# Rebuilt token attention in a two-block transformer kernel: two score regions per lane, and the short key pieces of a differential step issued side by side

## The reference, cut to what matters

```
mod = silu(c) @ w_ada[l] + b_ada[l]          # shifts, scales, gates
A: p = softmax(q k^T * scale);              o = p v
B: p = softmax(q k^T * scale + window_bias); o = p v      # bias on the 512 token keys
C: p = softmax(q1 k1^T) - lam * softmax(q2 k2^T); o = rms_norm(p v) * g_sub   # differential
x  = x + gate * (concat(oa, ob, oc) @ w_out[l])
```

## Time and profile before

| | |
|---|---|
| median of 3 runs | 3680.66 us (3677.1 to 3681.37) |
| span of the profiled execution | 3674.5 us (the profile has no other time of this execution) |
| PE busy | 3542.3 us, 96% of the span |
| DVE, ACT, POOL busy | 47%, 42%, 40% |
| token attention, layer 0 and layer 1 | 241.7 to 475.6 us and 1346.6 to 1574.3 us |
| context attention, layer 0 | 521.9 to 586.1 us |

### The profile page before, as it was taken

The page is one execution under the profiler, slowest core; times in us unless marked ns, Lnnn a source line. Parts: engine busy times, 40 slices in busy tenths (PEclk is TensorE's granted clock), DMA queues, the critical chain, the costliest instruction groups (busy, mean ns, idle before and its releaser), DMA issues.

```text
span 3674.5 us, 50083 instructions
## 1 busy us (share of the span) xinstructions
PE 3542.3 (96%) x19796; PEld 2813.1 (77%) x19796; DVE 1740.4 (47%) x2922; ACT 1525.6 (42%) x2558; POOL 1458.9 (40%) x986
## 2 busy tenths in 40 slices
PE   7999898999999999899999989999999989999998
PEld 5776566888899776578887768878887768888886
DVE  5766634433344766633542686161114676162114
ACT  4445544433355446534332355443223345443222
POOL 4520023544488520035444435344444434434442
PEclk8999998999999999999999999999999999999999
DMA  7613512333365421523333213223333212313331
GB/s 229 159 48 116 172 47 69 98 98 96 94 183 173 122 54 36 161 84 97 98 95 98 75 35 100 85 71 97 97 96 79 75 41 81 103 58 102 94 98 58
DMA packets 642466, 355.59 MB, mean 97 GB/s; under 512 B 70469, under 2 KB 614841, under 8 KB 642233
## 3 DMA queue, kind: packets, MB, share of 16 engines
q1 hardware_dynamic: 630379, 339.66, 32.0%
q10 hardware_dynamic: 11854, 12.72, 1.2%
...
## 4 chain that ended last, share of the span: by engine, by line
PE 89%; DVE 5%; ACT 3%; issue 2%; DMA 1%; POOL 1%; SPq 0%; ACTq 0%; DVEq 0%
PE psum L850 68%; PE psum L1055 5%; PE psum L1088 3%; PE psum L1106 2%; PE psum L874 1%; DVE neg_max L1920 1%; ACT work L1507 1%; PE psum L1135 1%; PE psum L954 1%; PE psum L878 1%; PE psum L1010 1%; PE psum L905 1%; PE psum L897 1%; DMA w_ada_first<-in_w_ada_dram 1%; PE psum L1113 1%
## 5 line engine op out<-in xcount | busy, mean ns | idle before, releaser
L833 POOL TENSOR_TENSOR w_lo<-w_raw,w_hi 128x256 fp32r<-128x256 f32 (+3 forms) x936 | 1397.0, 1512 | 2140.3 <-ACT w_hi L1358 2139.9
L850 PE MATMUL psum<-h_hi,w_hi 128*128 128x512 f32 (+1 forms) x2864 | 1078.7, 377 | 2.5 <-POOL w_lo L833 1.5
L850 PE MATMUL psum<-h_lo,w_hi 128*128 128x512 f32 (+1 forms) x2864 | 1054.5, 368 | 0.0
L850 PE MATMUL psum<-h_hi,w_lo 128*128 128x512 f32 (+1 forms) x2864 | 1054.1, 368 | 0.0
L1358 ACT ACTIVATE w_hi<-w_raw 128x1024 fp32r<-128x1024 f32 (+1 forms) x546 | 570.9, 1047 | 651.3 <-PE psum L850 618.2
L850 PEld LDWEIGHTS psum<-h_hi,w_hi 128*128 128x128 f32 x2864 | 541.5, 189 | 115.4 <-issue 20.2
L850 PEld LDWEIGHTS psum<-h_lo,w_hi 128*128 128x128 f32 x2864 | 541.5, 189 | 97.3 <-issue 9.9
L850 PEld LDWEIGHTS psum<-h_hi,w_lo 128*128 128x128 f32 x2864 | 541.3, 189 | 89.7
L850 PE MATMUL psum<-hid_hi,w_hi 128*128 128x512 f32 (+1 forms) x1040 | 393.0, 378 | 2.2 <-POOL w_lo L833 1.6
L850 PE MATMUL psum<-hid_lo,w_hi 128*128 128x512 f32 (+1 forms) x1040 | 391.9, 377 | 0.0
L850 PE MATMUL psum<-hid_hi,w_lo 128*128 128x512 f32 (+1 forms) x1040 | 391.9, 377 | 0.0
...
## 6 DMA issues: line engine op xcount, KB each, us to landing
w_raw<-in_w_up_dram SPq DMA_DIRECT2D x132, 512.0 KB, 3.8
w_raw<-in_w_ff_dram SPq DMA_DIRECT2D x128, 512.0 KB, 3.9
w_raw<-in_w_in_dram SPq DMA_DIRECT2D x92, 512.0 KB, 3.9
w_raw<-in_w_ada_dram SPq DMA_DIRECT2D x80, 512.0 KB, 4.2
w_raw<-in_w_down_dram SPq DMA_DIRECT2D x48, 512.0 KB, 3.6
w_raw<-in_w_mkv_dram SPq DMA_DIRECT2D x32, 512.0 KB, 3.8
...
```

Of the source, the lines that this page charges most:

```text
L833: m = nc.gpsimd.tensor_tensor(WL[:, c % NSPLIT, k:k + step, :], RAW[:, c % NRAW, k:k + step, :], WH[:, c % NSPLIT, k:k + step, :].bitcast( ...
L850: m = pe.matmul(out_ap, lhs(a, k), rhs(b, k), start=(k == 0 and n == 0), stop=(k == nk - 1 and n == 2))
```

## The change

The token attention gets a plan and loops of its own, `attention_plan_x` and `attend_x` on PE, ACT and DVE. What it does:

- The steps' order is A, C, B (before: A, B, C).
- Each lane has three PSUM banks that hold two regions of 768 columns, used in turn by even and odd steps. The 512-column piece (`score_long`) of step i+1 is issued at the end of PE's step i, the 256-column piece (`score_short`) at the start of step i+1, for both lanes side by side, after the exponentials of both lanes of step i.
- Transposed tiles of kinds A and B go into the step's own region (8 tiles) and bank 7 (4 tiles). In kind C each step is mixed and transposed two steps later through bank 7, four tiles and then two; the turn's values come three steps after its last step.
- Reciprocals are turned, copied and applied for every turn, no longer per group of four.
- The `w_ada` chunks are cut 256 columns by four contraction tiles, two of them a block; a step takes both and the next step turns the block. Layer l's own 32 chunks lie in steps 0 to 15 of its token attention, the 16 of layer 1's first part in steps 0 to 15 of layer 0's context attention, one to a step.
- The window is added to the bias tables on POOL instead of DVE. The norm of the differential heads is made beside the kind B steps.
- The context attention uses one output bank instead of two, and splits its first two output weights itself.

```diff
-            add(("ada", l, b, j), "w_ada", l, 2 * j, 2, [(0, 4 * P, 4 * P * b)])
+            add(("ada", l, b, j), "w_ada", l, 4 * j, 4, [(0, 2 * P, 2 * P * b)])
...
-    if key[0] != "att" or key[1] != "x":
+    if key[0] != "att" or step < 0:
         return []
-    l = key[2]
-    parts = [(l, b, j) for b in range(ADA_FIRST, 12) for j in range(4)]
-    if l == 0:
-        parts += [(1, b, j) for b in range(ADA_FIRST) for j in range(4)]
-    pair = step - ADA_LAST + len(parts) // 2
-    return parts[2 * pair:2 * pair + 2] if pair >= 0 else []
+    if key[1] == "x":
+        parts = [(key[2], b, j) for b in range(2 * ADA_FIRST, 24) for j in range(2)]
+        return parts[2 * step:2 * step + 2]
+    return [(1, b, j) for b in range(2 * ADA_FIRST) for j in range(2)][step:step + 1]
...
+            S = ("att", "x", layer)
+            n = len(steps)
+            diffs = [o for o, g in enumerate(groups) if g["diff"]]
+            turned_at, pv_at = {}, {}
+            for i, st in enumerate(steps):
+                turned_at.setdefault(i + (2 if st["diff"] else 1), []).append(i)
+            for q, u in enumerate(turns):
+                u["pv_at"] = u["after"] + (3 if steps[u["after"]]["diff"] else 2)
+                pv_at.setdefault(u["pv_at"], []).append(q)
+            ada_at, side = {}, {}
+            for i in range(n):
+                for block in ada_last(S, i):
+                    ada_at[i + 1] = block
+            for o in diffs:
+                side[groups[o]["last"] + 5] = ("sum", o)
+            std_at = groups[diffs[-1]]["last"] + 6
...
+        def region(i, m):
+            lane = PS[:, 3 * m:3 * m + 3, :].rearrange("p b c -> p (b c)")
+            return lane[:, i % 2 * NK:i % 2 * NK + NK]
+        def keys_long(i):
+            return slice(0, SEQ) if i % 2 == 0 else slice(CTX, NK)
+        def keys_short(i):
+            return slice(SEQ, NK) if i % 2 == 0 else slice(0, CTX)
...
+            def attend_x(att, before, before_second):
...
+                def score_long(i):
+                    if i == 0:
+                        for signal in before:
+                            pe.wait_ge(*signal)
+                    elif i == 1:
+                        pe.wait_ge(*before_second)
+                    elif steps[i - 2]["diff"]:
+                        pe.wait_ge(*at("exp_done", (S, i - 2, 1)))
+                    else:
+                        pe.wait_ge(*at("pt_copied_act", (S, i - 2)))
+                        pe.wait_ge(*at("pt_copied_dve", (S, i - 2)))
+                    for m, (q, k) in enumerate(steps[i]["lanes"]):
+                        ins = pe.matmul(region(i, m)[:, keys_long(i)], q, k[:, 0:SEQ], start=True, stop=True)
+                    ins.then_inc(*mark("long_done", (S, i)))
+                def score_short(i, lanes):
+                    if i:
+                        pe.wait_ge(*at("exp_done", (S, i - 1, lanes[-1])))
+                    for m in lanes:
+                        q, k = steps[i]["lanes"][m]
+                        pe.matmul(region(i, m)[:, keys_short(i)], q, k[:, SEQ:NK], start=True, stop=True).then_inc(
+                            *mark("scores_done", (S, i, m)))
...
+                def turn_mixed(i, fill):
+                    if fill:
+                        pe.wait_ge(*at("pt_copied_act", (S, i, 0)))
+                    else:
+                        pe.wait_ge(*at("mix_step", (S, i, "mixed")))
+                        if steps[i - 1]["diff"]:
+                            pe.wait_ge(*at("pt_copied_act", (S, i - 1, 1)))
+                        else:
+                            pe.wait_ge(*at("rest_copied_dve", (S, i - 1)))
+                    for n, kt in enumerate(range(4 * fill, min(4 * fill + 4, KEYS))):
+                        ins = pe.transpose(PS[:, 7, n * P:(n + 1) * P], probs(i, 1)[:, kt * P:(kt + 1) * P], IDENT)
+                    ins.then_inc(*mark("group_turned", (S, i, fill)))
...
+                score_long(0)
+                for i in range(att["length"]):
+                    turned = att["turned_at"].get(i, ())
+                    plain = [j for j in turned if not steps[j]["diff"]]
+                    mixed = [j for j in turned if steps[j]["diff"]]
+                    if i in att["ada_at"]:
+                        turn_ada(i)
+                    if i < len(steps):
+                        score_short(i, (0, 1))
+                    for j in mixed:
+                        turn_mixed(j, 0)
+                    for j in mixed:
+                        turn_mixed(j, 1)
+                    for j in plain:
+                        turn_plain(j)
+                    out_free(i)
+                    if i in att["side"]:
+                        side(i)
+                    for q in att["pv_at"].get(i, ()):
+                        value(q)
+                    ada(S, i, ada_rows, X_SIDE)
+                    if i + 1 < len(steps):
+                        score_long(i + 1)
...
+            def attend_x(att):
...
+                def recips(i):
+                    for block in ada_last(S, i):
+                        act.wait_ge(*at("w_used", IDS["ada", block[0], block[1], 1][0]))
+                        if ada_rows:
+                            act.wait_ge(*at("ada_turned", ada_rows[-1]))
+                        nc.scalar.activation(AROW[:, :], X_SIDE, ACT.Copy).then_inc(*mark("ada_rows", block))
+                        ada_rows.append(block)
+                    for q in att["pv_at"].get(i, ()):
+                        act.wait_ge(*at("pv_done", (S, q)))
+                        if q >= 2:
+                            act.wait_ge(*at("o_step", (S, q - 2)))
+                        nc.scalar.activation(recip_rows(q), X_RECIP, ACT.Copy).then_inc(*mark("recip_copied", (S, q)))
...
+                    if i == att["std_at"]:
+                        act.wait_ge(*at("side_taken", (S, i - 1)))
+                        nc.scalar.activation(SUBS[:, :, :], SUBS[:, :, :], ACT.Sqrt, bias=EPSC[:, 0:1],
+                                             scale=1.0 / HEAD).then_inc(*mark("sub_std", S))
+                n = len(steps)
+                for i in range(att["length"]):
+                    if 0 < i <= n and not steps[i - 1]["diff"]:
+                        copy_plain(i - 1)
+                    if i < n:
+                        exp(i, 0)
+                    if 2 <= i < n + 2 and steps[i - 2]["diff"]:
+                        copy_mixed(i - 2, 1)
+                    if 0 < i <= n and steps[i - 1]["bias"]:
+                        copy_rest(i - 1)
+                    beside(i)
+                    if i < n:
+                        exp(i, 1)
+                    if 0 < i <= n and steps[i - 1]["diff"]:
+                        copy_mixed(i - 1, 0)
+                    recips(i)
+                    if n - 4 <= i < n - 4 + AHEAD:
+                        split(IDS["out", "x", S[2]][i - n + 4])
...
+            def attend_x(att):
...
+                def scaled(q):
+                    u = turns[q]
+                    o, t = u["group"], u["t"]
+                    if t == 0 and o >= 2 and not groups[o]["diff"]:
+                        dve.wait_ge(*(at("side_taken", (S, groups[o - 2]["last"] + 5)) if groups[o - 2]["diff"] else
+                                      at("o_lo", (S, o - 2))))
+                    dve.wait_ge(*at("recip_copied", (S, q)))
+                    nc.vector.tensor_tensor(x_out(att, o)[:, t * P:(t + 1) * P], X_OUT, recip_rows(q), ALU.mult).then_inc(
+                        *mark("o_step", (S, q)))
...
+                for i in range(att["length"]):
+                    if l == 0 and i == 2:
+                        lam_ends()
+                    if i in att["ada_at"]:
+                        take_ada(i)
+                    if i < n:
+                        largest(i, 0)
+                        largest(i, 1)
+                    if 0 < i <= n and not steps[i - 1]["diff"]:
+                        copy_plain(i - 1)
+                        if not steps[i - 1]["bias"]:
+                            copy_rest(i - 1)
+                    if 0 < i <= n:
+                        sums(i - 1)
+                    for q in att["pv_at"].get(i, ()):
+                        scaled(q)
+                    if i + 1 < n and steps[i + 1]["bias"]:
+                        bias(i + 1)
...
+                    if c == IDS["qkv", "x", l][-1] + 1:
+                        pool.wait_ge(*at("tab_in", ("win", l)))
+                        for h in range(B_HEADS):
+                            nc.gpsimd.tensor_tensor(TB[:, h], TB[:, h], WINDOW.unsqueeze(1).broadcast_to([P, 14, 64]),
+                                                    ALU.add).then_inc(*mark("win_bias", (l, h)))
```

363 lines of the change are left out of this document (289 added, 74 removed).

## The result

The changed kernel takes 3774.85 us (median of 4 runs, 3773.92 to 3779.22), the kernel before 3681.01 us beside it (4 runs): ratio 1.0261, 95% interval 1.0246 to 1.0276. The forecast was 3721 us, range 3687 to 3748. It is slower, as forecast, by 94 us instead of 40.

The account below looks back on a forecast made before the run. PE, busy 91 and 90% in the token attentions, was taken as the bound. Token attentions +12.4 and +18.6 and context attention +9 made +40.0 on span 3674.5; plus 6.2 to the runs' median, 3721 us, range 3687 to 3748.

Parts of the forecast that it names:

- A steps: Steps 2 to 15 of both token attentions: PE, with chunks and half a turned block in each, sets 6.25 us.
- The hold: Odd C steps: DVE's scaling waits for ACT's late reciprocals copy, so the next maxima start at 2.45 us; step 5.95.
- B steps: Token attention steps 35 to 39: DVE's order gives 5.7 us each; with norm work and step 37's table loads, sum 34.2.
- The context attention: Chunks and turned blocks add 8.3 us in 12 steps, about 1 in four waiting C steps: +9, bounds +4 and +16.
- the clock term: Token attention's C steps: a clock of 0.91 over about 42 us that go by PE alone adds 4 us per layer.
- odd C steps longer than even ones: Sign that the forecast is right, token attention steps 20 to 31: odd steps 5.95 us, even ones 4.8.
- rival 3: Clock falls in the C steps to 0.79 and stays, context attention's late chunks at half clock: +20 and +7, 3748; chance 0.15.
- steps 32 to 34: Token attention, where B begins and the last C turns end: 5.55, 7.4 and 6.8 us, sum 19.8.
- Costed at nothing: Window additions on POOL, chunk transfers, the context attention's single output bank and the moved output-weight splits: no time added.
- Rival 1: The held DVE costs nothing in odd C steps: 26 us less in all, 3695 us; chance 0.15.
- rival 2: C and B steps go by DVE's own work, 3.5 and 4.5 us, not waits: 77 us less, 3644; chance 0.12.
- Rival 4: Modulation hidden in A steps: 14 steps at 5.8 us give 3708; chance included in the forecast's 0.58.

Follow-up runs that it names:

- e1: Changed kernel with ACT's copy of a turn's reciprocals ahead of its copy of the next mixed tiles: 3723.9 us.
- e2: Changed kernel with four unused PE matmuls in each of seven odd steps (19 to 33) of each token attention: 3745.8 us.
- e7b: e1 with token attention's chunks in steps 12 to 27, context attention's 16 in layer 0's steps 4 to 11, no output-weight splits in context attention: 3718.4 us.
- e8: e1 with token attention's chunks in steps 12 to 27 and, from step 18, their block turned behind the first four transposes: 3677.0 us.
- e15: e8 with ACT's copy of the reciprocals back behind the copy of the mixed tiles, as in the changed kernel: 3758.2 us.
- e12: e8 with the values of the last C turn in PE's step 33 instead of 34: 3665.6 us.

## Why the prediction was right and wrong

**Right.** *A steps*: 6.34 us against 6.25, PE without gaps; the double buffer brings nothing there. *The hold* and its place: shown by e1 and e2, and its length, 5.99 us for the odd step's 5.95. *Steps 16 to 19*: by the short pieces 19.8, as computed. *A C pair with the clock up*: 10.4 for 10.75 (e2, granted clock 0.91). *B steps*: 5.7, and 8.4 with the table load, as computed. *The context attention*: +11.7 for +9, and the single output bank costs nothing (e7b). *Transfers*: a `w_ada` chunk landed in 3.9 us and no A step waited for one. *The first, last and B parts* of layer 0 together: 50.6 us by the reciprocals and the stage's ends, for 50.1.

**Wrong: the clock term.** Layer 0's token attention came out 28.2 us above its 246.3, and the step that failed is "at a clock of 0.91 ... that is 4 us more". By the reciprocals on DVE:

```profile
363.04 0.15 DVE L2345 RECIPROCAL recip_sums<-prob_sums 128x2 f32<-128x2 f32 x1
...
449.95 0.15 DVE L2345 RECIPROCAL recip_sums<-prob_sums 128x2 f32<-128x2 f32 x1
```

The twelve intervals of C steps from 363.04 to 449.95 are 86.9 us where the sum had 65.1: +21.8. The three where B begins are 29.6 where it had 19.8: +9.8. The rest differs by 0.6 in all, less the 4 already taken for the clock: 28.2. What failed is the level: 0.62 was granted, not 0.91. The share of work that scales held: 42 us × (1 / 0.62 - 1) would have been 25.7 us, near the 21.8. It lies in the even steps alone, 8.44 us each for the predicted 4.8; so the sign "odd C steps longer than even ones" did not come true in the changed kernel, only in e2. Even rival 3 went no lower than 0.79, the mean of two windows of the earlier trace rows. These rows held a hint that was read past: in the kernel before, the last chunk of layer 1 is issued at 1540.93 us (line 954), the clock from 1472 to 1526 is 1.00, and in the second of those windows, behind the last chunk, it is 0.74. Then, hold, missing modulation and clock were added as if each stood alone, where the square of e1, e8 and e15 shows that they don't add. The order of the two sentences was the warning: the prediction worked out that PE would have 6.4 us of work in 10.75 and then chose a clock near full. By the Trainium skill, "TensorE: Matmul & The Clock Gate", section "What's actually happening", the clock is released by activity; e2, where work that nobody uses makes the kernel 29 us faster, agrees.

**Wrong: steps 32 to 34**, "6.8 (two turns of values)": the wait between the two turns on one output bank was left out, 3.6 us; from short pieces to short pieces step 34 takes 12.6 us, and 11.6 in e1 at the higher clock. e12 measured 11 us for both layers. The other two of the three steps are 3.1 us over. **Wrong, small**: 6.2 us were added from span to run, but the changed kernel's profiled execution took 3775.05 us with its span of 3773.0, 2 us apart; the rest was that the profiled execution of before was one of the shorter ones. In the prediction's reading of the kernel before, a sixth of layer 0's chunks, 8 of 48, lies in A steps and not a quarter; no term rests on it.

**Costed at nothing** were the splits and the bias on POOL. No run takes the bias back, and the splits of the context attention went out only together with its chunks (e7b), so neither is shown to be free.

**The rivals.** Rival 1 (the hold costs nothing) is refuted, and so is rival 2 for the changed kernel, whose C steps take 7.2 us on average; e8 shows that the new loops without hold, with the modulation in the C steps, reach 224.2 us in layer 0's token attention (241.81 to 466.04) against 233.9, and the context attention's chunks give it back. Rival 3 was the mechanism, at half the size that came: it had 27 us over the forecast, and 54 came. Rival 4 (A steps under PE's sum) is refuted.

What stays open: how the added time of the context attention divides into chunks, turned blocks and splits, and how much of the gain from e15 to e8 is the clock's and how much the row's wait.
